# A decoder layer's two feed-forwards: gate and up as seven block products, tokens in two halves, rounds unrolled

## The chip, the cores and the metric

The kernel runs on one core of a Trainium2 chip. The metric is the device time of one execution in microseconds (us); lower is better. The work of a core is split over TensorE (PE: matrix products, with the weight loads as rows of their own, PEld), VectorE (DVE), ScalarE (ACT), GpSimd (POOL) and SyncE (SP: issues transfers). The engines run their own instruction lists in order and meet at semaphores (`wait_ge`, `then_inc`).

## The reference

One layer of a hybrid decoder for 1024 prompt tokens and 64 sample tokens (together NT = 1088), model width D = 1024. The change is about the two feed-forwards that open and close the layer, each with D_FF = 2816:

```
x += 0.5 * SwiGLU(rms(x))
gate, up = split(rmsnorm(x, g) @ w_in, 2)      # w_in: 1024 x 5632
SwiGLU   = (silu(gate) * up) @ w_out           # w_out: 2816 x 1024
```

Between them lie the projection of x into the inputs of three branches (sparse attention, a gated recurrence, attention to a memory), the branches, and their merge by `w_out`. These parts stay, but for the norm in front of the projection and the order of the merge's last products.

## The kernel before

All activations lie transposed in SBUF: `x[:, k, t]` holds feature 128k+partition of token t, k = 0 to 7 (KT = 8). The tokens stand in three chunks `CH` of 364, 362 and 362 columns. Products keep float32 accuracy by splitting each factor into a rounded high part and a remainder: `products` (L325) issues three matmuls for each 128x128 block of weights, `w_hi*a_hi`, `w_hi*a_lo`, `w_lo*a_hi`, and sums them in PSUM.

`Feed` (L336) is a feed-forward. A Fori loop has G = 11 rounds; a round makes 256 of the 2816 inner features as two tiles t = 0, 1 and then multiplies by the two matching blocks of `w_out`:

- Weights come in six units of 128x1024 (gate and up of tile 0, of tile 1, two blocks of `w_out`). SP loads unit u into `raw` slot u % 3, ACT rounds it into `w_hi` (`high_part`, L472), POOL subtracts, `w_lo = raw - w_hi` (`low_part`, L386).
- `unit` (L397) on PE: for each chunk, 8 values of k times three matmuls, into PSUM banks 0 to 2 (gate) or 3 to 5 (up). A tile has 2 x 3 x 24 = 144 matmuls.
- `dve_products` (L507) on DVE scales the two by the tokens' inverse root (`sg`, `up`, one PSUM operand each), multiplies after ACT's silu (`pr`, both operands in SBUF) and, after ACT's rounding into `a_hi`, subtracts for `a_lo` (both in SBUF).
- `down` (L431): 24 groups (3 chunks x 8 rows j) of 6 matmuls, 144 in a round, each added into x by `dve_add` (L547), one PSUM operand and one in SBUF.

The norm does not stand in front of the products: `h_hi` and `h_lo` are x times gain, split; the inverse root (`Rooted`, `RootedWhole`, `RootedTiles`, L194 to L323) is worked out meanwhile and multiplied in behind. The norm in front of the projection, `NormBehind`, squares and sums each chunk after the last `dve_add` of its rows. The order is written out by hand on each engine; there is no planner.

## Time and profile before

| | |
|---|---|
| median of 3 runs | 3192.61 us (3187.55 to 3192.62) |
| span of the profiled execution | 3181.2 us |
| what the median has around the span | 11.4 us |
| mean granted TensorE clock | 0.986 of full speed |
| HBM read, written | 226.20 MB, 37.05 MB (83 GB/s over the span) |

The span reaches from the first to the last instruction of one execution; the runs' times are of other executions and take in what lies around it. No time of its own is given for the profiled execution beside its span. A group's "mean" is that of one instruction; matmuls overlap, so that the distance between their starts, not their duration, is what one costs. "Idle before" is the time that the engine stood before these instructions, with what ended it.

### The profile page before, as it was taken

To read this page: it belongs to the slowest core of one execution; us is meant where nothing else is said; L and a number is where in the kernel's file an instruction comes from. 1 tells how busy PE (TensorE), PEld (TensorE's weight loads), DVE (VectorE), ACT (ScalarE), POOL (GpSimd) and SP (SyncE) were. 2 spreads that over 40 slices of the span, in tenths; PEclk is the share of its full clock that TensorE was granted. 3 is DMA by queue.
4 is the path that set the end of the run, shared out by engine and by line. 5 is a ranking of instruction groups with operands and counts; after the bars stand their busy time and mean duration, and the time that the engine had idled before them with its cause. 6 is when DMAs were issued, how large, how long until landed. Compare 5 with 4: busy or idle time off the path is not lost. (4 is left out here: it accounts for less than half of the span.)

```text
span 3181.2 us, 51686 instructions
## 1 busy us (share of the span) xinstructions
PE 3076.4 (97%) x19690; PEld 2901.0 (91%) x19690; DVE 1736.2 (55%) x3041; ACT 911.5 (29%) x1616; POOL 667.9 (21%) x415
## 2 busy tenths in 40 slices
PE   8999999999899999999899999999999999999999
PEld 8999999999899999999756666679999999999998
DVE  6333333333669999999635666655544333333333
ACT  5111111111433333333344545441232111111111
POOL 2112221221453421133250000012112122121120
PEclk9999999999999999999989999999999999999999
DMA  3111111111223222222346556444421111111111
GB/s 117 47 40 40 53 41 45 46 40 47 86 77 92 86 74 86 61 74 66 100 159 207 179 171 203 151 161 144 130 61 41 46 46 40 46 46 40 40 49 60
DMA packets 256495, 265.47 MB, mean 83 GB/s; under 512 B 14575, under 2 KB 197458, under 8 KB 256334
## 3 DMA queue, kind: packets, MB, share of 16 engines
q1 hardware_dynamic: 250858, 254.61, 25.6%
q0 software_dynamic: 4128, 4.20, 0.5%
q10 hardware_dynamic: 1348, 4.49, 0.4%
q8 instruction: 103, 1.69, 0.2%
q14 instruction: 58, 0.48, 0.0%
HBM read 226.20 MB, written 37.05 MB: 83 GB/s over the span
## 5 line engine op out<-in xcount | busy, mean ns | idle before, releaser
L331 PE MATMUL bank<-h_hi,w_hi 128*128 128x362 f32 (+1 forms) x3384 | 1118.6, 331 | 19.6 <-DVE h_lo L218 6.4
L331 PE MATMUL bank<-h_lo,w_hi 128*128 128x362 f32 (+1 forms) x3384 | 1112.9, 329 | 0.0
L331 PE MATMUL bank<-h_hi,w_lo 128*128 128x362 f32 (+1 forms) x3384 | 1111.7, 329 | 0.0
L331 PEld LDWEIGHTS bank<-h_hi,w_hi 128*128 128x128 f32 x3384 | 638.3, 189 | 26.8 <-issue 11.9
L331 PEld LDWEIGHTS bank<-h_lo,w_hi 128*128 128x128 f32 x3384 | 638.8, 189 | 2.7
L331 PEld LDWEIGHTS bank<-h_hi,w_lo 128*128 128x128 f32 x3384 | 638.6, 189 | 0.0
L388 POOL TENSOR_TENSOR w_lo<-raw,w_hi 128x1024 fp32r<-128x1024 f32 x132 | 316.1, 2403 | 1267.3 <-ACT w_hi L483 1267.3
L553 DVE SCALAR_TENSOR_TENSOR x<-bank,x 128x362 f32<-128x362 f32 (+1 forms) x528 | 279.8, 534 | 212.1 <-PE bank L331 211.9
L331 PE MATMUL bank<-a_hi_ffn,w_hi 128*128 128x362 f32 (+1 forms) x1056 | 347.7, 329 | 7.3 <-DVE x L553 5.6
L331 PE MATMUL bank<-a_lo_ffn,w_hi 128*128 128x362 f32 (+1 forms) x1056 | 346.4, 328 | 0.0
L331 PE MATMUL bank<-a_hi_ffn,w_lo 128*128 128x362 f32 (+1 forms) x1056 | 346.2, 328 | 0.0
L516 DVE TENSOR_TENSOR sg_ffn<-bank,drs_ffn 128x364 f32<-128x364 f32 x132 | 70.3, 535 | 388.0 <-PE bank L331 387.6
L521 DVE TENSOR_TENSOR up_ffn<-bank,drs_ffn 128x364 f32<-128x364 f32 x132 | 70.6, 535 | 370.0 <-PE bank L331 370.0
L483 ACT CAST w_hi<-raw 128x1024 fp32r<-128x1024 f32 x132 | 135.8, 1044 | 428.6 <-PE bank L331 428.6
L1313 POOL TENSOR_TENSOR w_lo<-raw,w_hi 128x1024 fp32r<-128x1024 f32 x53 | 129.6, 2444 | 392.5 <-ACT w_hi L1537 392.5
L331 PEld LDWEIGHTS bank<-a_hi_ffn,w_hi 128*128 128x128 f32 x1056 | 198.4, 188 | 10.0 <-DVE x L553 7.8
L331 PEld LDWEIGHTS bank<-a_lo_ffn,w_hi 128*128 128x128 f32 x1056 | 198.5, 188 | 0.1
L331 PEld LDWEIGHTS bank<-a_hi_ffn,w_lo 128*128 128x128 f32 x1056 | 198.5, 188 | 0.0
L499 ACT CAST a_hi_ffn<-pr_ffn 128x364 fp32r<-128x364 f32 x132 | 65.6, 497 | 432.5 <-DVE pr_ffn L528 432.5
L3066 POOL TENSOR_TENSOR w_lo<-raw,w_hi 128x1024 fp32r<-128x1024 f32 x20 | 50.0, 2503 | 606.0 <-ACT w_hi L3115 606.0
L493 ACT ACTIVATE sg_ffn<-sg_ffn 128x364 f32<-128x364 f32 x132 | 66.7, 508 | 384.0 <-DVE sg_ffn L516 383.9
L1902 DVE MAX8 top<-S 128x8 f32<-128x384 f32 (+5 forms) x192 | 171.1, 891 | 4.1
(371 smaller groups left out, 4105.2 us busy)
## 6 DMA issues: line engine op xcount, KB each, us to landing
raw<-in_w_ffn_in SPq DMA_DIRECT2D x88, 512.0 KB, 3.8
k_ring<-in_cache_k SPq DMA_DIRECT2D x128, 256.0 KB, 3.9
v_ring<-in_cache_v SPq DMA_DIRECT2D x128, 256.0 KB, 4.3
raw<-in_w_in SPq DMA_DIRECT2D x53, 512.0 KB, 4.8
raw<-in_w_ffn_out SPq DMA_DIRECT2D x44, 512.0 KB, 3.5
kept_g<-stage SPq DMA_DIRECT2D x24, 544.0 KB, 3.1
gate<-kept_g SPq DMA_DIRECT2D x24, 544.0 KB, 3.6
x<-x_kept SPq DMA_DIRECT2D x8, 544.0 KB, 4.5
```

Of the source, the lines that this page charges most:

```text
L331: mm = pe.matmul(out, left, right, start=(start and i == 0 and j == 0), stop=(stop and i == n - 1 and j == 2))
L388: pool.tensor_tensor(self.w_lo[:, u % 3, :], self.raw[:, u % 3, :], self.w_hi[:, u % 3, :].bitcast(F32), ALU.subtract).then_inc(self.low, 1)
L483: act.copy(self.w_hi[:, u % 3, :], self.raw[:, u % 3, :]).then_inc(self.high, 1)
L493: act.activation(self.sg[:, c, 0:w], self.sg[:, c, 0:w], ACT.Silu).then_inc(self.silu_done, 1)
L499: act.copy(self.a_hi[:, t, t0:t0 + w], self.pr[:, c, 0:w]).then_inc(self.prod_high, 1)
L516: dve.tensor_tensor(sg[:, c, 0:w], bank[c][:, 0:w], rs[:, t0:t0 + w], ALU.mult).then_inc(self.scaled, 1)
L521: dve.tensor_tensor(up[:, c % 2, 0:w], bank[3 + c][:, 0:w], rs[:, t0:t0 + w], ALU.mult).then_inc(self.up_scaled, 1)
L553: dve.scalar_tensor_tensor(self.x[:, j, t0:t0 + w], bank[:, 0:w], 0.5, self.x[:, j, t0:t0 + w], ALU.mult, ALU.add).then_inc(self.x_added, 1)
L1313: pool.tensor_tensor(w_lo[:, n % 3, :], raw[:, n % 3, :], w_hi[:, n % 3, :].bitcast(F32), ALU.subtract).then_inc(low, 1)
L1902: after(dve.max(top8[0:rows, :], scores))
L3066: pool.tensor_tensor(w_lo[:, n % 3, :], raw[:, n % 3, :], w_hi[:, n % 3, :].bitcast(F32), ALU.subtract).then_inc(low, 1)
```

## The change

The tokens are taken in two halves, `HV`: 512 tokens as two column blocks of 256, then 576 as two of 288. All 11 rounds are run for the first half, then for the second (ROUNDS = 22, written out, no loop), so every weight is loaded and split twice.

For a tile, gate and up are one 2x2 block product: rows gate and up, inner halves k = 0 to 3 and 4 to 7, columns the two token blocks. It is made with seven block products in place of eight (the form with 4 + 4 operand sums and 7 sums of results). The four sums of activation blocks (T1 to T4) are made once for each half, by DVE, with their high and low parts (`Operands`; three of the seven low parts by POOL). These operands are of the fully normed x, so the inverse root is needed before the first product. The four sums of weight blocks (S1 to S4, 128x512 each) are made for each tile by DVE (`combine`). The weights are split in 18 pieces of 512 columns for each round (7 + 7 + 4), through a ring of 10. The results are put together by an ACT copy (`first_copy`) and seven DVE additions (`post`), each with one PSUM operand. `down` has 8 rows j, each of two column blocks, 96 matmuls in a round.

The norm before the projection does its first chunk during the last rounds, the merge's last products are split 512, 288, 288 and reordered, four of the nine row tiles of the result are written during the second feed-forward's second half, and the start transposes and squares tile by tile.

```diff
+HV = [(0, 256), (512, 288)]
+OPS = 7
+B11, T2, B21, T3, T1, T4, B22 = range(OPS)
+PIECES = 18
+A11, S2, A12, S3, S1, A22, S4 = range(OPS)
+BANK_OF = (0, 1, 0, 1, 3, 2, 3)
+FIRST = (0, 4, 1, 2, 3, 5, 6)
+POSTS = 7
+POST_OF = (1, 2, 3, 4, 4, 5, 6)
...
+    def high_part(self, act, p):
...
+        if p >= self.RING:
+            i0, n0 = divmod(p - self.RING, PIECES)
+            if n0 < 14:
+                act.wait_ge(self.multiplied, self.after(2 * i0 + n0 // OPS, n0 % OPS))
+            else:
+                act.wait_ge(self.out_ready, KT * i0 + (4 if n0 < 16 else 8))
+        act.copy(self.ring_hi[p % self.RING], self.source(p)).then_inc(self.high, 1)
+    def low_part(self, pool, p):
+        pool.wait_ge(self.high, p + 1)
+        pool.tensor_tensor(self.ring_lo[p % self.RING], self.source(p), self.ring_hi[p % self.RING].bitcast(F32),
+                           ALU.subtract).then_inc(self.low, 1)
+    def combine(self, dve, g, m):
...
+        if g:
+            dve.wait_ge(self.low, self.piece(g - 1, m) + 1)
...
+        dve.tensor_tensor(s(m), left, right, op).then_inc(self.combined, 1)
+    def product(self, pe, g, n):
...
+        pe.wait_ge(self.low, p + 1)
...
+        if n == 2:
+            pe.wait_ge(self.first_copied, g + 1)
+        elif n == 3:
+            pe.wait_ge(self.posted, POSTS * g + 1)
+        elif n == 6:
+            pe.wait_ge(self.posted, POSTS * g + 5)
...
+    def on_act(self, act, hooks):
...
+                for n in range(OPS):
+                    if n == 0:
+                        self.first_copy(act, g)
+                    elif n == 2:
+                        self.silu(act, g, 0)
+                    elif n == 6:
+                        self.act_prod_high(act, g, 0)
+                        self.silu(act, g, 1)
+                        self.act_prod_high(act, g, 1)
+                    hooks(act, i, t, n)
+                    self.high_part(act, at + n)
...
+    def tile_on_dve(self, dve, g, ahead):
+        some = (lambda m: self.combine(dve, g + 2, m)) if ahead else (lambda m: None)
+        self.post(dve, g, 0)
+        some(S3)
+        self.post(dve, g, 1)
+        some(S1)
+        self.post(dve, g, 2)
+        some(S2)
+        self.post(dve, g, 3)
+        self.post(dve, g, 4)
+        some(S4)
+        self.post(dve, g, 5)
+        self.gate_up(dve, g, 0)
+        self.post(dve, g, 6)
+        self.prod_low_part(dve, g, 0)
+        self.gate_up(dve, g, 1)
+        self.prod_low_part(dve, g, 1)
...
+    def on_dve(self, dve, hooks, before_adds, after_add):
+        for i in range(self.ROUNDS):
+            self.tile_on_dve(dve, 2 * i, True)
+            self.tile_on_dve(dve, 2 * i + 1, False)
+            hooks(dve, i)
+            turn = i == self.G - 1
+            if turn:
+                self.next_half_early(dve)
+                self.next_half(dve)
+            for m in (S3, S1, S2):
+                self.combine(dve, 2 * i + 3, m)
...
+            for j in range(KT):
+                self.add(dve, i, j)
...
+                if j == 4 and not turn:
+                    self.combine(dve, 2 * i + 3, S4)
```

In `on_dve`, `next_half_early` and `next_half` make the second half's operands: eight scalings of 576 columns, and sums and low parts of 1152 columns, of which the later ones stand between and behind the eight additions of the round.

## Rows read from the trace of the kernel before

**Rows 1.** The page: busy time of each engine, share of the span, instructions

```profile
PE 3076.4 (97%) x19690; PEld 2901.0 (91%) x19690; DVE 1736.2 (55%) x3041; ACT 911.5 (29%) x1616; POOL 667.9 (21%) x415
```

**Rows 2.** Tile a_hi_ffn, two rounds: count, ns min/median/max, first and last start

```profile
L331 PE MATMUL bank<-a_hi_ffn,w_hi x48: 323/329/330, 291.1 to 314.6; 128*128 128x362 f32 x32, 128*128 128x364 f32 x16
...
L331 PE MATMUL bank<-a_hi_ffn,w_hi x48: 322/329/330, 721.7 to 745.1; 128*128 128x362 f32 x32, 128*128 128x364 f32 x16
```

**Rows 3.** Timeline of TensorE, 256 columns: start us, duration us

```profile
1671.82 0.28 PE L331 MATMUL bank<-w_hi,m_lo 128*128 128x256 f32 x1
...
1673.50 0.28 PE L331 MATMUL bank<-w_hi,m_hi 128*128 128x256 f32 x1
```

**Rows 4.** Busy time, clock and DMA in six stretches

```profile
core 0: us, PE busy (x) PEld busy (x) DVE busy (x) ACT busy (x) POOL busy (x), PEclk, DMA share, GB/s
315.00:386.70 71.70, 71.70 (x434) 71.70 (x433) 25.17 (x48) 11.81 (x18) 14.35 (x6) 1.00 0.15 44
47.50:50.00 2.50, 0.79 (x4) 0.29 (x3) 2.47 (x3) 1.89 (x3) 0.00 (x0) 1.00 0.00 0
824.50:842.00 17.50, 10.84 (x46) 9.45 (x45) 14.06 (x16) 7.43 (x14) 8.75 (x7) 0.71 0.50 144
2267.00:2270.00 3.00, 0.88 (x6) 0.58 (x4) 2.93 (x7) 0.99 (x2) 0.00 (x0) 1.00 1.10 342
2270.00:2275.00 5.00, 4.14 (x16) 4.14 (x17) 2.23 (x5) 1.44 (x2) 2.37 (x1) 0.66 0.29 73
2364.50:2378.00 13.50, 8.00 (x28) 6.79 (x27) 12.94 (x18) 4.16 (x5) 4.96 (x2) 0.62 0.27 78
```

**Rows 5.** Groups by form (mean ns last before the bar), one by line (min/median/max)

```profile
L388 POOL TENSOR_TENSOR w_lo<-raw,w_hi 128x1024 fp32r<-128x1024 f32 x132 | 316.1, 2403 | 1267.3 <-ACT w_hi L483 1267.3
...
L483 ACT CAST w_hi<-raw 128x1024 fp32r<-128x1024 f32 x132 | 135.8, 1044 | 428.6 <-PE bank L331 428.6
...
L553 DVE SCALAR_TENSOR_TENSOR x<-bank,x 128x362 f32<-128x362 f32 x352 | 188.0, 534 | 161.3 <-PE bank L331 161.2
...
L2540 DVE COPY kt<-bank 128x512 f32<-128x512 f32 x64 | 44.3, 691 | 66.3 <-PE bank L2732 66.3
...
L1554 ACT CAST qq<-qi 64x512 fp32r<-64x512 f32 x12 | 7.4, 614 | 0.2
...
L2306 DVE RECIPROCAL mk_rs<-mk_rs x1: 6552/6552/6552, 1653.4 to 1653.4; 128x1024 f32<-128x1024 f32 x1
```

**Rows 6.** Lines L3189, L528 and L553: ns min/median/max, who waited

```profile
L3189 DVE TENSOR_TENSOR m_lo<-m,m_hi x24: 527/531/2445, 2224.8 to 2271.2; 128x362 fp32r<-128x362 f32 x16, 128x364 fp32r<-128x364 f32 x8
...
  PE bank L331: 3.0, 1
...
L528 DVE TENSOR_TENSOR pr_ffn<-sg_ffn,up_ffn x132: 535/536/2717, 55.9 to 3141.9; 128x362 f32<-128x362 f32 x88, 128x364 f32<-128x364 f32 x44
...
L553 DVE SCALAR_TENSOR_TENSOR x<-bank,x x528: 520/535/538, 80.2 to 3170.6; 128x362 f32<-128x362 f32 x110, 128x364 f32<-128x364 f32 x66
```

**Rows 7.** Timelines of VectorE and GpSimd at 2224 us

```profile
2224.81 2.38 DVE L3189 TENSOR_TENSOR m_lo<-m,m_hi 128x364 fp32r<-128x364 f32 x1 [0.96 <-PE bank L331]
...
2224.39 2.40 POOL L3066 TENSOR_TENSOR w_lo<-raw,w_hi 128x1024 fp32r<-128x1024 f32 x1 [10.19 <-ACT w_hi L3115]
```

**Rows 8.** GpSimd line L985, and VectorE's timeline while it runs

```profile
L985 POOL TENSOR_TENSOR nss_mix<-nss_mix,nsq_mix x18: 827/973/1121, 799.9 to 842.8; 128x362 f32<-128x362 f32 x12, 128x364 f32<-128x364 f32 x6
...
842.96 1.16 DVE L1026 TENSOR_TENSOR h_lo<-nhn_mix,h_hi 128x362 fp32r<-128x362 f32 x1
```

**Rows 9.** Tiles h_hi and a_hi_ffn: both feed-forwards' first and last products

```profile
L331 PE MATMUL bank<-h_hi,w_hi x96: 322/329/609, 18.2 to 73.2; 128*128 128x362 f32 x64, 128*128 128x364 f32 x32
...
L331 PE MATMUL bank<-a_hi_ffn,w_hi x48: 322/329/605, 794.4 to 824.2; 128*128 128x362 f32 x32, 128*128 128x364 f32 x16
...
L331 PE MATMUL bank<-h_hi,w_hi x96: 321/329/674, 2367.7 to 2423.0; 128*128 128x362 f32 x64, 128*128 128x364 f32 x32
...
L331 PE MATMUL bank<-a_hi_ffn,w_hi x48: 322/329/412, 3142.1 to 3169.9; 128*128 128x362 f32 x32, 128*128 128x364 f32 x16
```

More of the change, by code:

```diff
@@ new lines, in on_pe, with first_copy @@
+    def on_pe(self, pe, hooks, after_down):
+        for i in range(self.ROUNDS):
+            for t in range(2):
+                for place, n in enumerate(self.order(2 * i + t)):
+                    hooks(pe, i, t, place)
+                    self.product(pe, 2 * i + t, n)
+            self.down(pe, i, after_down if i == self.ROUNDS - 1 else None)
+    def first_copy(self, act, g):
+        i, t = divmod(g, 2)
+        w = HV[self.half(i)][1]
+        act.wait_ge(self.multiplied, self.after(g, 0))
+        if g:
+            act.wait_ge(self.posted, POSTS * (g - 1) + 2)
+        act.copy(self.s1[:, 0:w], self.bank[4 * t][:, 0:w]).then_inc(self.first_copied, 1)
```

1306 lines of the change are left out of this document (757 added, 549 removed).

## The prediction

> **What bounds the kernel now.** I read the page's busy times first: TensorE is busy 97% of the span, VectorE 55%, ScalarE 29%, GpSimd 21% [rows 1]. Then the windows by stage: in a steady round of the feed-forward PE has no gap at all (71.70 of 71.70 us, clock 1.00, which is 2.4 GHz), with DVE at 25.2 us, ACT at 11.8 and POOL at 14.4 [rows 4]. So there the time is that of the matmuls' issue, and nothing else. Six rounds take 721.7 - 291.1 = 430.6 us, 71.77 us each; with 432 matmuls in a round that is 0.1661 us for one of 362.67 columns [rows 2]. The two feed-forwards run from 18.2 to 824.2 us and from 2367.7 to 3169.9 [rows 9], 806 and 802 us; 11 rounds are 789.5, so 16.5 and 12.7 are their own starts and ends.
>
> **The matmuls.** What does a narrower one cost? The trace has the same triple of products with 256 columns: 14 steps in 1.68 us, 0.120 us each [rows 3]. It doesn't stop falling at 256, and the line through both points (0.43 ns a column, 9 ns fixed) gives 0.1338 us for 288. Gate and up: before 2 x 11 x 2 x 144 = 6336 matmuls, 1052.4 us; after 2 x 44 tiles x 84 = 7392, half at 0.120 and half at 0.1338, 938.0 us: **-114.4 us**, 10.9% and not 12.5%, since the fixed part is paid on more instructions. Down: before 3168, 526.2 us; after 2 x 22 x 96 = 4224, 536.0 us: **+9.8**. If nothing waits, the change is worth -104.6 us. A round is then 31.7 us (256) or 35.3 (288).
>
> **What the other engines get.** In these 31.7 us POOL has 18 subtractions of 512 columns. The trace has 362 columns at 0.827 us undisturbed and 1024 at 2.40 [rows 5, 8]; between them lies 1.18 us, so 21 us, 67% where it had 20%. DVE has 14 posts (0.42 us, from 0.534 for 362 and 0.691 for 512 [rows 5]), 8 combines of 512 (0.69), 8 products and low parts (0.42) and 8 additions of 512 (0.69): 20.3 us. ACT has 18 copies of 512 (0.61) and 10 of about 0.4 (from 0.614 and 1.044): 15 us [rows 5]. No engine is full. But the sums must not be read alone, for one thing that before hid by its timing.
>
> **DVE behind POOL.** The line m_lo L3189 takes 0.53 us in the median and 2.445 at most, L528 0.535 and 2.717 [rows 6]. Beside POOL's timeline: POOL starts at 2224.39 for 2.40 us, DVE's m_lo starts at 2224.81 and ends at 2227.19, 0.40 us after POOL's end [rows 7]. The same with short POOL instructions: 1.16 for 0.53 [rows 8]. The additions L553, whose one operand is PSUM, never exceed 0.538 in 528 [rows 6]. So a DVE instruction with both operands in SBUF that starts while POOL runs waits until POOL's instruction is done, then needs about its columns' time; and PE did wait for it (3.0 us [rows 6]). That this is so in general the Trainium skill says in "SBUF — State Buffer", Who interferes with whom: a DVE instruction with two SBUF inputs and a GpSimd instruction that reads SBUF share a port, and the second blocks fully; the trace agrees. Before, a round has 12 such DVE instructions and POOL runs 20% of the time. After, it has 16 in half the time, POOL runs 67%, and two of the combines wait for POOL's semaphore just when POOL goes on with its next piece.
>
> **A round by hand (256 columns, 0 = first product).** The end of down frees pieces 8 and 9; POOL does 8 to 11 back to back until 2.1, 3.3, 4.5 and 5.65. DVE's combine S3 overwrites the sum that piece 10 reads, is released at 4.5, meets piece 11 in POOL and ends at 5.65 + 0.55 = 6.2. Behind it: post 1 (6.6), silu (7.0), ACT's high part of 12 (7.5), POOL's 12 and 13 (9.1, 10.3). S4 is released by 13, meets 14 (until 11.45), ends 12.0; post 5 12.4; gate_up meets 15 and ends 13.2; post 6 13.6, silu 14.0, gate_up 14.5, ACT's rounding 14.95, high part of 16 15.5, and only then, in ACT's order, first_copy of tile 1: 15.8. PE started product 6 at 8.95 in place of 8.64 (post 4 late: 0.3), has done tile 1's products 0 and 1 at 13.3, and waits for the copy: **2.6 us**. In down the additions come behind three combines and cost another 0.5. Together 3.4 us in a round of the first half. With 288 columns PE is slower and the chain hardly: 0, 1.7 and 0.3, together 2.0. For 2 x 11 pairs of rounds: 22 x 5.4 = **+119 us**. PE has more work than this chain everywhere else; second tiles have no combines inside.
> Bounds: without DVE's waits behind POOL the same chain ends at 13.6 and costs 0.75 a round of 256 and 0.1 of 288, +19 us; with every hop 0.1 us longer and the waits a whole POOL instruction each, 4.8 and 3.2, +176 us.
>
> **The turn between the halves (twice).** Behind the last tile of half 1, DVE does 8 scalings of 576 columns (0.72 each, by the row of 512), a sum and a low part of 1152 (1.3 each), the three combines, 13.5 us in all since PE's last gate product, and only then the first addition that down's fifth group (due at 5.8) waits for: 8.5 us. The new half's first tile needs each 1152-column sum, high and low part in turn, some with POOL (2.7 each): 5 us more than a usual one. And a gap of 3 us on PE is followed by half clock: 0.66 over the 5 us from 2270, 0.62 over the 13.5 us from 2364.5 that begin with such a gap (the lower level is 1.2 GHz), while a gap of 2.2 us at 47.5 leaves it at 1.00 [rows 4]; here that is worth some 3.5 us. Together 17, **+34 us** (20 to 50).
>
> **Starts, seams, the rest.** First feed-forward: the first product now needs root, reciprocal (6.55 us for 1024 columns [rows 5], so 3.3 for 512), scaling, sum, high and low: at about 26 us, not 18.2 [rows 9], and the tile is some 7 us longer; together 15, and 4 for the projection's norm inside the last additions, against 16.5: **+2**. Second: first product some 4 us after the merge, a tile 8 us longer and 5 of slow clock, against 12.7 and the 3 us in front of it: **+1**. At the projection's start PE stands 6.7 of 17.5 us at clock 0.71 [rows 4], some 12 us lost; its first chunk's norm is now ready: **-8**. These are worth -20 to +20 together. The transfers double for the feed-forwards, to some 100 GB/s; windows with 342 exist [rows 4], each unit is asked for 15 us ahead: nothing. No loop: the instruction fetch lies under PE's work as it does in the projection, which is straight code: nothing.
>
> **Sum:** -104.6 + 119 + 34 - 5 = +43 us. Against the profiled execution's span of 3181.2 that is 3224; the median of the runs stands 11.4 above that span, so **3236 us**.
>
> **Rivals.**
> *A, the forecast:* PE waits for first_copied some 2 to 3 us in each round. Likeliest's own range 3205 to 3270. For it speak rows 6 to 8. Chance 0.45.
> *B, faster:* the waits of DVE behind POOL seldom fall on the chain to first_copy. Then 22 x 0.85 = 19 us of stalls, a turn of 12 each: 3192.6 - 104.6 + 19 + 24 - 5 = 3126. It decides from 3.4 us per pair of rounds: below it the kernel is faster. For it: in the whole trace of before few of such instructions are hit (medians 0.53 [rows 6]); against: POOL's share then and now. Chance 0.25.
> *C, the clock falls too:* the 2.6 us gap lies between 2.2 (kept) and 3 (lost). If each 256 round loses about 3.4 us at half clock, 1.7 us: 22 x 1.7 = +37, 3273. Chance 0.15. The Trainium skill ("TensorE: Matmul & The Clock Gate", HAM oscillation) tells of kernels in which each such wait is followed by half clock; no row of before shows a repeated one.
> *D, a longer chain:* the upper bound above, 8.0 us per pair: +176 in place of 119, 3293. Chance 0.15.
> That narrow matmuls aren't cheaper is excluded by rows 3.
>
> So slower by over 0.2% (which is about what a measurement of this kernel tells from no change) in A, C and D but for a little: 0.70; within 0.2% 0.05; faster 0.25. The range takes in B's centre and D with a margin: 3120 to 3320; about 0.1 is left below, 0.05 above.
>
> **What would show it.** Matmul starts 0.120 and 0.134 us apart; 7392 + 4224 in the feed-forwards. A PE wait of 1.5 to 3 us once in each round, released by ACT's first_copy; combines with a median near 1.2 us and posts at 0.42 to 0.46; rounds of 35 and 37 us; one hole of 8 us in each feed-forward's middle. The prediction is wrong if rounds are under 33 and 36 us, if the combines take 0.7 in the median, or if PE's clock falls in each round.

## The result, and the profile after

| | before | after |
|---|---|---|
| median of the runs | 3190.08 us (3186.04 to 3192.62, 4 runs) | 3425.39 us (3420.92 to 3428.33, 4 runs) |
| span of the profiled execution | 3181.2 us | 3422.8 us |
| mean granted TensorE clock | 0.986 | 0.951 |

The ratio is 1.0738 (95% interval 1.0723 to 1.0754). The forecast was slower, 3236 us, with a range up to 3320: the direction is right, the size is not. It said +43 us and the change costs 235 (242 between the two spans). The forecast also took 11.4 us as what stands around the span. The profiled execution of the changed kernel took 3424.36 us, only 1.6 above its span, so most of the 11.4 was the difference between two executions of the kernel before.

The page of the changed kernel, busy times; beside [rows 1] POOL's time has more than doubled and PE's share has fallen:

```profile
PE 3075.7 (90%) x21770; PEld 2870.5 (84%) x21802; DVE 2286.8 (67%) x3670; ACT 1281.6 (37%) x2445; POOL 1456.3 (43%) x1087
```

Windows of the changed kernel (rounds are counted from 0). They answer to [rows 4]: a steady round of 256 columns, one of 288, the second feed-forward's first round from its first product, the two rounds of its turn, and round 15 of the first feed-forward:

```profile
core 0: us, PE busy (x) PEld busy (x) DVE busy (x) ACT busy (x) POOL busy (x), PEclk, DMA share, GB/s
2743.10:2780.60 37.50, 33.82 (x267) 33.30 (x266) 23.10 (x38) 13.91 (x28) 24.07 (x18) 0.95 0.28 85
3069.20:3107.30 38.10, 36.02 (x270) 35.66 (x269) 24.50 (x38) 14.68 (x29) 23.73 (x18) 1.00 0.33 98
2529.70:2593.00 63.30, 42.70 (x269) 40.40 (x270) 48.05 (x54) 25.28 (x44) 45.21 (x28) 0.76 0.22 67
2930.80:2978.40 47.60, 36.47 (x267) 35.94 (x266) 33.13 (x50) 19.30 (x33) 20.76 (x16) 0.86 0.18 56
2978.40:3031.20 52.80, 41.35 (x267) 40.26 (x266) 33.17 (x42) 16.17 (x31) 36.34 (x24) 0.84 0.24 70
678.60:726.30 47.70, 40.10 (x266) 39.47 (x266) 28.13 (x38) 15.00 (x30) 27.46 (x20) 0.89 0.22 67
```

A round with nothing in its way takes 31.7 or 35.3 us. None does. The account of the 242 us, from the starts of each round's first product and of the stages' last products, beside the terms of the forecast:

| us | forecast | measured |
|---|---|---|
| products and `down` alone (taken over; run 1 bears it out) | -104.6 | -104.6 |
| steady rounds, over 31.7 and 35.3 | +101 | +211 |
| the turns' four rounds, over the same | +45 | +67 |
| starts, less before's own (30 in 806 and 802 us) | +10 | +66 |
| projection to merge | -8 | +5 |
| end | 0 | -2 |
| sum | +43 | +242 |

(The forecast's 5.4 us per pair of rounds are counted here in the row to which the round belongs. Steady rounds are the 38 that are neither first nor at a turn. Starts: the first feed-forward's first product stands at 40.4 in place of 18.2 us, the second's 12.0 behind the merge's last in place of 3.0, and the first rounds last 65.2 and 63.3 us from there.)

The forecast's chain is there. VectorE, GpSimd, ScalarE and TensorE at the end of the first tile of a round that begins at 2743.1 (columns: start us, duration us, in brackets the idle time ahead and what ended it):

```profile
2753.91 1.77 DVE L399 TENSOR_TENSOR sums_ffn<-raw,sums_ffn 128x512 f32<-128x512 f32 x1 [1.76 <-POOL w_lo L369]
2755.60 0.41 DVE L543 TENSOR_TENSOR up_ffn<-bank,u_ffn 128x256 f32<-128x256 f32 x1
2756.12 1.00 DVE L550 TENSOR_TENSOR sg_ffn<-sg_ffn,up_ffn 128x256 f32<-128x256 f32 x1
```

```profile
2753.85 2.99 POOL L369 TENSOR_TENSOR w_lo<-raw_ffn,w_hi 128x512 fp32r<-128x512 f32 x2
```

```profile
2758.39 0.40 ACT L498 CAST a_hi_ffn<-sg_ffn 128x256 fp32r<-128x256 f32 x1 [0.49 <-DVE sg_ffn L550]
2758.70 0.61 ACT L365 CAST more_hi_ffn<-raw_ffn 128x512 fp32r<-128x512 f32 x1
2759.22 0.36 ACT L483 COPY s_ffn<-bank 128x256 f32<-128x256 f32 x1
```

```profile
2759.73 0.36 PE L231 MATMUL bank<-op_hi_ffn,more_hi_ffn 128*128 128x256 f32 x1 [2.89 <-ACT s_ffn L483]
```

S4's combine starts 0.06 us behind GpSimd's piece and takes 1.77 us; `gate_up` takes 1.00; `first_copy` comes at 2759.22, 16.1 us into the round (forecast 15.8), and PE stands 2.89 us for it, 3.17 from start to start of its matmuls (forecast 2.6). With two more waits (product 6 and down's fifth group, 0.6 and 0.5 us longer than a matmul's step) and the clock at 0.95 the round lasts 37.5 us where 35.1 was forecast.

The combines of the changed kernel, ns min/median/max, to be set beside [rows 6]:

```profile
L399 DVE TENSOR_TENSOR sums_ffn<-raw x88: 674/688/1703, 25.1 to 3345.5; 128x512 f32<-128x512 f32 x88
...
L399 DVE TENSOR_TENSOR sums_ffn<-raw,sums_ffn x88: 681/1738/1771, 27.1 to 3372.7; 128x512 f32<-128x512 f32 x88
...
L399 DVE TENSOR_TENSOR sums_ffn<-raw_ffn x44: 671/1777/1786, 60.2 to 3366.8; 128x512 f32<-128x512 f32 x44
```

S4 (second line) is stretched in most places and tile 1's S1 (third line) in 36 of 44; of the first group one half is (S3 of tile 0, as forecast). What the forecast had not is how the wait is shared out: whichever instruction comes first keeps its time and the other engine's waits. In the rows above GpSimd's piece of 2753.85 keeps its 1.28 us, S4 behind it takes 1.77, and GpSimd's next piece, which meets S4, takes the rest of the 2.99. So GpSimd's 1.28 us become 1.5 to 1.75 as well wherever the two meet.

### The profile page after: what moved, and what is told of

The parts are those of the page before. It is cut to its first block and busy times, and to the rows that moved or that the text cites. A ratio compares the mean times of both kernels' runs of the same rounds, so it can differ in the third digit from the quotient of the medians.

```text
span 3422.8 us, 58318 instructions
## 1 busy us (share of the span) xinstructions
PE 3075.7 (90%) x21770; PEld 2870.5 (84%) x21802; DVE 2286.8 (67%) x3670; ACT 1281.6 (37%) x2445; POOL 1456.3 (43%) x1087
## 5 line engine op out<-in xcount | busy, mean ns | idle before, releaser
L231 PE MATMUL bank<-op_hi_ffn,w_hi 128*128 128x256 f32 (+1 forms) x1488 | 456.7, 307 | 137.1 <-ACT s_ffn L483 72.4
L231 PE MATMUL bank<-op_lo_ffn,w_hi 128*128 128x256 f32 (+1 forms) x1488 | 450.1, 302 | 0.0
L231 PE MATMUL bank<-op_hi_ffn,w_lo 128*128 128x256 f32 (+1 forms) x1488 | 448.8, 302 | 0.0
L231 PE MATMUL bank<-h_hi,w_hi 128*128 128x362 f32 (+1 forms) x1272 | 421.6, 331 | 8.9 <-ACT xp L1834 5.0
L231 PE MATMUL bank<-h_lo,w_hi 128*128 128x362 f32 (+1 forms) x1272 | 418.4, 329 | 0.0
L231 PE MATMUL bank<-h_hi,w_lo 128*128 128x362 f32 (+1 forms) x1272 | 418.0, 329 | 0.0
L3338 POOL TENSOR_TENSOR w_lo<-raw,w_hi 128x1024 fp32r<-128x1024 f32 x20 | 50.8, 2546 | 606.4 <-ACT w_hi L3391 606.4
L231 PEld LDWEIGHTS bank<-op_lo_ffn,w_hi 128*128 128x128 f32 x1488 | 303.8, 204 | 0.1
L231 PEld LDWEIGHTS bank<-op_hi_ffn,w_lo 128*128 128x128 f32 x1488 | 303.3, 204 | 0.0
L1575 POOL TENSOR_TENSOR w_lo<-raw,w_hi 128x1024 fp32r<-128x1024 f32 x53 | 129.3, 2441 | 383.9 <-ACT w_hi L1801 383.8
L231 PEld LDWEIGHTS bank<-h_hi,w_hi 128*128 128x128 f32 x1272 | 240.5, 189 | 13.1 <-issue 5.8
```

The costliest lines, as they stand in the source:

```text
L231: mm = pe.matmul(out, left, right, start=(start and i == 0 and j == 0), stop=(stop and i == n - 1 and j == 2))
L1575: pool.tensor_tensor(w_lo[:, n % 3, :], raw[:, n % 3, :], w_hi[:, n % 3, :].bitcast(F32), ALU.subtract).then_inc(low, 1)
L3338: pool.tensor_tensor(w_lo[:, n % 3, :], raw[:, n % 3, :], w_hi[:, n % 3, :].bitcast(F32), ALU.subtract).then_inc(low, 1)
```

## The experiments

Runs are numbered as they stand here. Each stands beside runs of the kernel before on the same chip; its ratio is to those. Differences between versions are differences of ratios times 3187; where two intervals overlap, the difference is not shown by the times and rests on the gaps in the traces alone.

### What a steady round waits for

**1. The lock itself**, that is DVE's waiting for GpSimd's reads. GpSimd writes what it otherwise computes.

```diff
-        pool.tensor_tensor(self.ring_lo[p % self.RING], self.source(p), self.ring_hi[p % self.RING].bitcast(F32),
-                           ALU.subtract).then_inc(self.low, 1)
+        pool.memset(self.ring_lo[p % self.RING].bitcast(F32), 0.0).then_inc(self.cleared, 1)
+        pool.wait_ge(self.cleared, p + 1)
+        pool.memset(self.ring_lo[p % self.RING].bitcast(F32), 0.0).then_inc(self.low, 1)
```

> Edit: POOL's low parts of the weights are left out; in their place POOL clears the 512 columns twice (two memsets, together about as long, 1.1 us for 1.3, but reading nothing from SBUF). Theory 1 (DVE instructions with two SBUF operands wait for POOL instructions that read SBUF): combine's median falls from about 1.7 to 0.69 us, S4 ends 2.5 us earlier, rounds 34 us (256, clock kept) and 36.5 (288): about -100 us, near 3325. Theory 2 (DVE is slow or late for another reason, POOL only in its own queue): combine keeps its duration, and less than 20 us is gained.

3204.01 us, ratio 1.0054 (1.0033 to 1.0075): 218 us less than the changed kernel, twice what theory 1 had. A steady round of each kind, and the combines:

```profile
core 0: us, PE busy (x) PEld busy (x) DVE busy (x) ACT busy (x) POOL busy (x), PEclk, DMA share, GB/s
2588.60:2620.40 31.80, 31.80 (x267) 31.76 (x265) 19.15 (x38) 14.09 (x28) 18.40 (x36) 1.00 0.33 100
2875.30:2910.90 35.60, 35.60 (x271) 35.60 (x270) 20.48 (x38) 14.96 (x29) 18.47 (x36) 1.00 0.35 105
```

```profile
L401 DVE TENSOR_TENSOR sums_ffn<-raw,sums_ffn x88: 681/683/694, 27.0 to 3155.6; 128x512 f32<-128x512 f32 x88
```

PE is busy without a gap, so 264 matmuls cost what the forecast gave them (0.120 and 0.134 us each), at twice the transfers' rate of before. POOL is still busy 58% of the round, now with writes of 0.53 us, and no combine is stretched: GpSimd's reading is what DVE waits for. This is what the Trainium skill says ("SBUF — State Buffer", Who interferes with whom): a DVE instruction with two SBUF inputs contends with one of GpSimd that reads, not with one that only writes. But POOL's chain is also shorter here (1.05 us a piece for 1.28 or more), so this run takes away the lock between the engines and the length together; run 4, with GpSimd's work unchanged, parts them.

**2. ScalarE's order.** Tile 1's `first_copy` is issued ahead of silu 1 of tile 0.

```diff
                         self.act_prod_high(act, g, 0)
+                        if t == 0:
+                            self.first_copy(act, g + 1)
                         self.silu(act, g, 1)
```

> Edit: in tile 0 of each round ACT issues tile 1's first_copy ahead of silu 1 and of the last rounding, not behind them and piece 16's high part. Theory 1 (PE's wait of 3.17 us at tile 1's third product is ACT's order, fed by the DVE chain): the wait falls under 1 us, PE's clock no longer falls in the 256 rounds, rounds go from 37.5 to about 33.5 us (256) and from 38.1 to 36 (288): about -120 us, near 3305. Theory 2 (the chain is long whatever ACT does): the wait moves to tile 1's fourth product, which needs post 0 behind the last low part, or into down; then 35.5 and 37.5, about -50 us.

3409.33 us, 1.0701 (1.0680 to 1.0722): -12. The wait for the copy falls from 3.17 to 1.4 us, and waits of 0.6 us at the next product and 2.4 us (from 0.64) at down's fifth group take its place. That is less than either theory had: the 256 rounds of the second feed-forward take 36.6 us, or 38.1 where half clock follows the new wait (five of nine). The queue ahead of the copy is not the cause; DVE is late with everything behind it.

**3. DVE's order.** Each combine one or more posts later, S4 at the tile's end.

```diff
         self.post(dve, g, 0)
-        some(S3)
         self.post(dve, g, 1)
-        some(S1)
+        some(S3)
         self.post(dve, g, 2)
-        some(S2)
+        some(S1)
...
-        some(S4)
+        some(S2)
...
         self.prod_low_part(dve, g, 1)
+        some(S4)
```

> Edit: on DVE, combine S3 stands behind post 1, S1 behind post 2, S2 behind post 4, S4 behind the tile's last low part; nothing else is changed. Theory 1 (S3 and S4, which wait for POOL's semaphore and then for its next piece, hold up the posts): post 5 starts when its product is done, the wait at tile 1's third product falls from 3.17 to about 1 us, rounds 34 (256) and 36 us (288): -110 us. Theory 2 (the time is DVE's total): S4 now delays tile 1's post 0, and the wait appears at tile 1's fourth product: about -30 us.

3331.18 us, 1.0455 (1.0433 to 1.0477): -90 by four moved lines, near theory 1's 110. Rounds of 34.7 and 36.8 us; the wait for the copy is 1.2 us and the clock stays at 1.00 in all steady rounds of the second feed-forward. The combines still meet GpSimd; they only no longer stand in front of a post or a product that PE waits for.

**4. Operands in PSUM.** The same arithmetic, but tile 0's `up` and gated product stay in banks that are free by then (post 4 into the bank of products 1 and 3, post 5 and `gate_up` in place; `gated` gives bank 2 or 1 for tile 0, `sg` for tile 1), so that four DVE instructions have one PSUM operand in place of two in SBUF.

```diff
+        if t == 0 and n in (4, 5):
+            to = self.bank[1 if n == 4 else 2][:, 0:w]
...
+        at = self.gated(g, c)
+        up = self.up[:, c * w:(c + 1) * w] if g % 2 else at
+        dve.tensor_tensor(at, sg, up, ALU.mult).then_inc(self.prod_done, 1)
```

> On the changed kernel, same arithmetic. Tile 0's up values and gated products are left in PSUM (post 4 into the bank of the third product, post 5 in place, gate times up in place), so that the four DVE instructions of tile 0 behind silu (two gate_up, two low parts) have one PSUM operand and should not wait for GpSimd. Theory 1, DVE behind GpSimd on the chain to tile 1's first_copy: gate_up 1.0 and 1.0 become 0.42, the PE wait in front of tile 1's third product falls from 3.17 us to under 2.0 in the rounds of 256 columns and the clock no longer falls there; round 37.5 to 35 us, 288 columns 38.07 to 37.3: -50 to -70 us, 3365. Theory 2, the combines alone set the chain: gate_up is not what is late, the gap stays over 2.8 us and the time falls by less than 15 us.

3385.18 us, 1.0625 (1.0607 to 1.0643): -36, between the two theories. `gate_up` of both tiles, ns mean before the last bar:

```profile
L554 DVE TENSOR_TENSOR sg_ffn<-sg_ffn,up_ffn 128x256 f32<-128x256 f32 x44 | 22.9, 520 | 2.3
...
L554 DVE TENSOR_TENSOR bank<-sg_ffn,bank 128x256 f32<-128x256 f32 x44 | 18.9, 429 | 2.3
```

Tile 0's is 429 ns (0.60 us over both tiles before), under GpSimd's reads and at unchanged POOL work, so it is the operands' place that decides. The wait for the copy goes from 3.17 to 2.57 us, by the 0.57 that the one `gate_up` on its chain had lost (1.00 to 0.43). Two neighbouring rounds with this wait, one at full clock and one not:

```profile
core 0: us, PE busy (x) PEld busy (x) DVE busy (x) ACT busy (x) POOL busy (x), PEclk, DMA share, GB/s
2613.80:2649.70 35.90, 32.34 (x267) 31.82 (x266) 23.04 (x39) 13.85 (x28) 24.04 (x19) 1.00 0.30 90
2649.70:2686.60 36.90, 33.83 (x267) 33.31 (x266) 22.53 (x39) 13.87 (x28) 23.91 (x19) 0.95 0.29 87
```

In this run the wait of 2.55 to 2.57 us is followed by 3.4 us at half clock in 13 of the 16 rounds that have it, and such a round is 1.0 us longer.

**5. Both, 3 and 4.** No other edit.

> The kernel of the run with the combines moved later (3331 us) with tile 0's up values and gated products in PSUM as well, same arithmetic. Theory 1: both remove different waits behind GpSimd on the same chain; the 1.20 us gap in front of tile 1's third product falls to about 0.3 and the round of 256 columns from 34.7 to about 33.7, that of 288 from 36.8 to 36.0: -32 us, 3299. Theory 2: with the combines late, the chain is no longer bound there but by the additions at down's fifth group (1.45 us), which then grow: -10 us or less, 3321 or more.

3288.48 us, 1.0328 (1.0311 to 1.0345): -40 against run 3, a little more than theory 1 had. The steady rounds:

```profile
core 0: us, PE busy (x) PEld busy (x) DVE busy (x) ACT busy (x) POOL busy (x), PEclk, DMA share, GB/s
2552.50:2586.10 33.60, 32.17 (x266) 31.80 (x265) 23.43 (x38) 14.06 (x28) 24.88 (x18) 1.00 0.32 95
2952.10:2987.90 35.80, 35.80 (x271) 35.64 (x270) 23.20 (x38) 14.84 (x29) 24.58 (x18) 1.00 0.35 104
```

With all of POOL's reading left in, rounds of 288 columns have no wait over 0.3 us, and those of 256 have 1.44 us in front of down's fifth group and 0.55 at product 6.

### The first feed-forward's norm

**6 and 7.** GpSimd's sums left out but for one column (run 6), and the whole sums at another place (run 7):

```diff
+        m = 1 if c == 0 else w
-        pool.tensor_tensor(self.ss[:, t0:t0 + w], self.ss[:, t0:t0 + w], self.sq[:, n % 3, 0:w], ALU.add
+        pool.tensor_tensor(self.ss[:, t0:t0 + m], self.ss[:, t0:t0 + m], self.sq[:, n % 3, 0:m], ALU.add
```

> On the changed kernel. GpSimd's seven sums of squares for the projection norm's first chunk, made during rounds 12 to 16 of the first feed-forward, add one column in place of 364; the rest of each sum is left out. Theory 1, GpSimd's time: the 5.1 to 5.5 us that PE stands in front of down's fifth group in rounds 13 to 16 come from GpSimd being about 1 us a sum late with the weights of the next pieces and from DVE's instructions behind these sums; without them the four gaps fall to 1 us or less and half of their half-clock time goes: 4 x (4.5 + 2.5) = 28 us, 3397. Theory 2, ScalarE: the squares on ScalarE (0.5 us each, two a round) and the wait for the additions keep the roundings back; the gaps stay over 4 us and the time is 3420 or more.

3413.01 us, 1.0711 (1.0693 to 1.0729): -9, not told apart from the changed kernel by the times. The four gaps fall from 5.1 to 5.5 us to 4.2 and no further, so the sums' own time is the small part. Run 7 has what keeps them.

```diff
-        if n == 0 and 0 <= k < 4:
+        if n == 4 and 0 <= k < 4:
```

> On the changed kernel, same arithmetic. In rounds 13 to 16 of the first feed-forward GpSimd makes the norm's two sums ahead of the next round's piece 4 in place of piece 0. Theory 1, the order: in the trace of the changed kernel GpSimd stands idle from about 701 to 703.2 us with pieces 0 to 3 ready, since its next instruction is a sum that waits for ScalarE's squares, which stand in ScalarE's order behind the fifth product of tile 1; the four pieces come some 4 us late and every DVE instruction of tile 1 then meets GpSimd. With the sums at piece 4 the gap in front of down's fifth group falls from 5.5 to 1 to 2 us and most of the half clock goes: 4 x 6.5 = -26 us, 3399. Theory 2, the added work (two sums, two squares) is what costs: the gaps stay over 4 us and the time within 8 us of 3425.

3402.87 us, 1.0667 (1.0645 to 1.0690): -23. The gaps are 0.8 to 1.5 us, the rounds 38.5 to 40.8 in place of 44.0 to 47.7. GpSimd in the changed kernel had stood 5.6 us for ScalarE's squares:

```profile
703.22 2.29 POOL L1212 TENSOR_TENSOR nss_mix<-nss_mix,nsq_mix 128x364 f32<-128x364 f32 x2 [5.59 <-ACT nsq_mix L1204]
```

Pieces that ScalarE had rounded by then stood behind that wait, as theory 1 had it. Two sums of 1 us cost 8.5 us a round, 6.2 of it by where they stood.

### The turn and the starts

**8. GpSimd's share of the operands** left out, without a read:

```diff
+        if o in (B21, T4, B22):
+            eng.memset(self.lo[s][:, o, :, :].bitcast(F32), 0.0).then_inc(self.low[1], 1)
+            return
```

> On the changed kernel. GpSimd's three low parts of the activation operands (three for each half of each feed-forward, 12 in all) are left out: GpSimd clears the places by one memset each, without reading SBUF; the low parts of the weights stay. Theory 1, the lock in the starts and turns: GpSimd's 2.5 to 3.4 us instructions stretch DVE's sums and low parts of 1024 columns from 1.2 to 2.2 to 3.4 us, some five of them in a start and two or three in a turn. Then each start gets 6 to 8 us shorter with the clock and each turn 3: about -20 us, 3405. Theory 2: the starts are the chain of the operands itself on DVE (8 scalings, 4 sums, 4 low parts, 16 us alone) and GpSimd's weight pieces stretch it as much: the time falls by under 8 us.

3409.30 us, 1.0695 (1.0677 to 1.0713): -14. First rounds are 3.2 us shorter, the second round of each turn 5.1. Nearer theory 1, but a tenth of what starts and turns cost.

**9. Four additions ahead of the operands' second half** in the turn:

```diff
             for j in range(KT):
                 self.add(dve, i, j)
+                if turn and j == 3:
+                    self.next_half(dve)
+                    for m in (S3, S1, S2):
+                        self.combine(dve, 2 * i + 3, m)
```

> Edit: at the turn between the halves the first four additions of down stand ahead of the second four scalings and the three combines, and the sum T2 and low part T1 behind the fifth. Theory 1 (PE's 8.1 us gap in down at the turn is the additions behind the operand making): the gap falls to about 2.5 us, and 5 us are gained at each turn, -10 us. Theory 2 (DVE is the bound of the turn as a whole): the gap moves to the first products of the second half, less than 3 us gained.

3422.74 us, 1.0744 (1.0723 to 1.0764): nothing. The wait in `down` falls from 8.1 to 3.2 us and the round from 47.6 to 41.6; the next goes from 53 to 58.0 and 59.5. Theory 2: what one round wins the next one pays.

**10. Repairs together**: run 5, the sums at piece 4, and the 3.7 us reciprocal cut in two behind the additions of rounds 7 and 8.

```diff
-        if i == 8:
-            ops.dve_invert(dve, 1)
...
+            if i in (7, 8) and self.late_invert:
+                self.ops.dve_invert_part(dve, i - 7)
```

> Same arithmetic. The run with tile 0's products in PSUM and the combines late (3288 us), with the norm's sums at piece 4, and with the reciprocal for the second half (3.7 us on DVE ahead of round 8's additions) cut into two of 288 columns behind the additions of rounds 7 and 8, where DVE waits for the next tile. Theory 1: rounds 13 to 16 fall from 42.5 to 36 us and round 8 from 39.6 to 34: -30 us, 3258. Theory 2: the reciprocals now meet the next round's first posts and combines and the norm's sums the pieces behind them: -12 us or less, 3276 or more.

3261.13 us, 1.0231 (1.0207 to 1.0255): -31 against run 5. Rounds 13 to 16 take 36.4 us, round 8 33.6. What is left stands in starts and turns. The second feed-forward's start in this kernel, VectorE and then TensorE:

```profile
2450.15 3.74 DVE L180 RECIPROCAL op_rs_ffn<-op_rs_ffn 128x576 f32<-128x576 f32 x1
2453.81 0.62 DVE L410 TENSOR_TENSOR sums_ffn<-raw,raw_ffn 128x512 f32<-128x512 f32 x1
...
2456.54 0.42 DVE L556 TENSOR_TENSOR u_ffn<-bank,s_ffn 128x256 f32<-128x256 f32 x1
```

```profile
2457.10 0.55 PE L241 MATMUL bank<-op_hi_ffn,w_hi 128*128 128x256 f32 x1 [8.66 <-DVE u_ffn L556]
```

Post 0, which PE waits for, stands behind a reciprocal that is needed some 360 us later and behind four combines. In the turn ScalarE's `first_copy` stands behind the rounding of a late sum:

```profile
2843.48 2.21 ACT L215 CAST op_hi_ffn<-op_f_ffn 128x1152 fp32r<-128x1152 f32 x2 [6.61 <-DVE op_f_ffn L208]
...
2846.63 0.39 ACT L494 COPY s_ffn<-bank 128x288 f32<-128x288 f32 x1
```

**11. The order at these places** (reciprocal into rounds 7 and 8 in both feed-forwards; tile 1's combines behind posts 1 and 4; in the turn `first_copy` ahead of two roundings and S4 behind post 1):

```diff
-        ops.dve_invert(dve, 1)
-        for s in (S3, S1, S2, S4):
-            feed.combine(dve, 1, s)
...
+            if i == self.G - 1:
+                self.first_copy(act, 2 * self.G)
+                for o in (T3, B22):
+                    self.ops.act_high(act, 1, o)
```

> The repaired kernel (3261 us), same arithmetic, with only the order changed in each feed-forward's first tile and in the turn: the reciprocal of the second half stands behind the additions of rounds 7 and 8 in the second feed-forward too, tile 1's combines stand behind post 1 and post 4 in place of ahead of post 0, and in the turn ScalarE's first_copy stands ahead of two of the operands' roundings and S4's combine behind post 1. Theory 1, order: in the trace before it PE stands 8.9 us in front of the fourth-placed product of the second feed-forward, until post 0 at 2456.5, which stands behind a reciprocal of 3.7 us and four combines of 0.7; in the turn 5.8 us for first_copy at 2846.6, which stands behind the rounding of a sum that DVE makes late, and 3.3 us for post 0 behind S4's combine. Then the second start gets 6 us shorter, the first 3, each turn 6: -21 us, 3240. Theory 2, sheer DVE work: the combines and posts only change places, PE waits later in the same tile: -6 us or less.

3253.07 us, 1.0209 (1.0191 to 1.0227): -7, theory 2's number, with intervals that overlap. The 8.9 us at the fourth-placed product are 2.6 and the turn's 5.8 are gone, but 4.2 to 4.9 us stand in front of tile 1's fourth product, which waits for post 0 behind the combines that now stand at tile 0's end. The old order had been the cause of the wait; the new one made another.

**12. The additions ahead of three combines.**

```diff
-            for m in (S3, S1, S2):
+            for m in (S3, S1, S2) if turn else ():
...
                 self.add(dve, i, j)
+                if j in (1, 2, 3) and not turn:
+                    self.combine(dve, 2 * i + 3, (S3, S1, S2)[j - 1])
```

> The order-fixed kernel with the three combines S3, S1, S2 of the next round's second tile moved from ahead of down's additions to behind the second, third and fourth of them (not in the turn). Theory 1: the gap of 1.45 us in front of down's fifth group in the rounds of 256 columns is the time by which these combines, 1.7 us each behind GpSimd, make the first addition late; it goes: 17 x 1.3 and a few us from rounds 1 to 3, 13 to 16 and 20, -25 us against the order-fixed kernel. Theory 2: the combines now meet the next tile's first posts and products 6 and 9 wait for them: -8 us or less.

3214.40 us, 1.0095 (1.0076 to 1.0114): -36 against run 11, more than theory 1's 25. Steady rounds are 32.3 and 35.6 us:

```profile
core 0: us, PE busy (x) PEld busy (x) DVE busy (x) ACT busy (x) POOL busy (x), PEclk, DMA share, GB/s
2585.70:2618.00 32.30, 32.02 (x267) 31.82 (x266) 23.06 (x39) 14.06 (x28) 25.02 (x18) 1.00 0.33 99
2911.50:2947.10 35.60, 35.60 (x270) 35.60 (x269) 22.08 (x40) 14.84 (x29) 24.73 (x18) 1.00 0.30 90
```

POOL reads as much as ever and DVE is as busy as in the changed kernel (23.1 us). So 5.2 us of the changed kernel's 37.5 were order and the place of two operands, with the clock that followed.

**13. The combines that run 11 had put at the first tile's end**, spread over the second tile (the third place in which they stand):

```diff
+        elif g % (2 * self.G) == 1:
+            for m in (S3, S1, S2):
+                self.combine(dve, g + 1, m)
...
+        if g % (2 * self.G) == 1:
+            self.combine(dve, g + 1, S4)
```

> The run with the additions first (3214 us), same arithmetic, with the four combines for the third tile of each half moved from the end of the first tile to behind post 1 (three) and the last low part (one) of the second tile. Theory 1, order: the gap of 4.6 to 4.9 us in front of the fourth product of the second tile, which waits for post 0 behind these four combines (6.4 us behind GpSimd), goes in all four places: -4 x 4.5 = -18 us, 3196. Theory 2: DVE has no slack there and the wait moves on to the seventh product or to down: -6 us or less.

3200.98 us, 1.0058 (1.0041 to 1.0074): -12, between the theories. The gaps of 4.6 to 4.9 are gone; in their place come 0.6 to 2.4 us later on. The turn's second rounds fall from 50.1 and 50.3 us to 45.1 and 47.1.

**14. The turn's three combines behind its fifth addition.**

```diff
-            for m in (S3, S1, S2) if turn else ():
-                self.combine(dve, 2 * i + 3, m)
...
+                if turn and j == 4:
+                    for m in (S3, S1, S2):
+                        self.combine(dve, 2 * i + 3, m)
```

> The kernel with the combines spread, and in the turn the three combines that stand ahead of down's additions placed behind the fifth of them. Theory 1: the gap of 8.9 us in front of down's fifth group in the turn falls by their 2.1 us, and with the first_copy ahead it doesn't come back: -2 x 2 = -4 us. Theory 2, DVE is full in the turn (2817 to 2846 us in the trace of the repaired kernel without a pause): the next tile loses what down wins, within 2 us.

3200.12 us, 1.0048 (1.0034 to 1.0062): no change. The turn's first round is 2.6 to 2.9 us shorter and the second 2.1 to 4.1 longer. This order buys nothing in the turn; that of run 13 did.

### The clock by itself

**15.** Idle matmuls inside PE's waits, into the bank that the next product overwrites:

```diff
+            count = (30 if self.spare else 20, 8, 0, 25, 18, 0, 8) if g == 0 else (0, 0, 20, 10, 0, 0, 8)
+            for _ in range(count[n]):
+                pe.matmul(self.bank[BANK_OF[n]][:, 0:P], self.ops.ones[:, :], self.ops.ones[:, :], start=True, stop=True)
```

> The kernel of the run before in this list with idle matmuls (128x128 of ones, written to the bank that the next product then overwrites) issued on PE inside its waits: 20 and 30 ahead of the feed-forwards' first products, 18, 8, 25 and 8 ahead of four products of the first tile, and 20, 10 and 8 in the second half's first tile. Nothing else changes. Theory 1, the clock is a cost of its own: 37 to 43 us at half clock in each feed-forward's first round and 10 to 14 us in each of the two rounds of a turn give half of themselves back where PE, not the operands, is last; starts -8 each, turns -5 each: -26 us, 3232. Theory 2: in starts and turns DVE's operands are last until the first tile's end, so that a faster PE only waits longer: within 8 us of the kernel without the filler.

3265.10 us, 1.0240 (1.0213 to 1.0268), run 10 having 1.0231: no gain. The start and the turn's second round:

```profile
core 0: us, PE busy (x) PEld busy (x) DVE busy (x) ACT busy (x) POOL busy (x), PEclk, DMA share, GB/s
2414.30:2496.50 82.20, 63.33 (x474) 61.18 (x473) 59.53 (x69) 27.96 (x48) 45.81 (x28) 0.88 0.20 59
...
2842.20:2894.20 52.00, 46.21 (x343) 45.38 (x342) 32.62 (x42) 16.80 (x31) 37.37 (x24) 0.93 0.24 72
```

In run 10 the same two had clocks of 0.76 and 0.90 and lasted 77.6 and 51.5 us. In the turn the clock is up a little (3.4 us less at half clock) and the time is not shorter. The start shows nothing, by a fault of mine: the idle matmuls in front of the fourth-placed product stood behind its wait for post 0 and took 8.1 us there. Run 16 leaves them out.

**16.** On run 13's kernel, with idle matmuls only ahead of a feed-forward's first three products:

```diff
+            count = (30 if self.spare else 20, 8, 0, 0, 18, 0, 0) if g == 0 else (0,) * OPS
```

> The kernel of the run above with idle matmuls on PE only where an operand's low part is awaited: 20 or 30 ahead of a feed-forward's first product, 18 and 8 ahead of the next two. Theory 1, the clock: PE reaches the first tile's later products at full clock, 35 to 40 us of half clock a start become under 15, and since the later waits are shorter than before half of that is given back: -8 us a start, -16 us against the run above. Theory 2: operands are still last until the first tile's end; what is gained is the second tile and down at full clock only: -4 us or less.

3196.60 us, 1.0040 (1.0026 to 1.0054) beside 1.0058 (1.0041 to 1.0074) for run 13: not to be told apart, where theory 1 had -16. First rounds 74.5 and 74.2 us beside 75.1 and 73.1, though the half clock in them fell from 37 and 31 us to 19 and 17. Theory 2: DVE's operands are last until the first tile's end; a faster PE waits longer.

**17. The bound without the lock**: run 15 with the weights' low parts left out:

> The filler kernel with the weights' low parts left out (GpSimd clears each place twice by memset in their place, without reading SBUF). It bounds what is left of the lock between DVE and GpSimd in the repaired kernel. Theory 1: rounds of 256 columns fall from 33.6 to 31.8 us (18 of them), those of 288 from 35.8 to 35.2 (20), starts by 5 us each: -55 us against the filler kernel, about 3180, so that starts and turns alone then eat the 105 us that the products save. Theory 2: the repairs have already removed nearly all of the lock's cost: less than 25 us below the filler kernel.

3201.36 us, 1.0043 (1.0030 to 1.0056): -63 against its filler kernel, theory 1's number and more. Rounds are of 31.7 and 35.1 to 35.6 us. Even so it is not faster than before, and run 13, with all of the work in it, has since come as far.

**18. The last version**: run 16 with DVE's side work behind the additions and silu's table loaded in a pause.

```diff
-            hooks(dve, i)
             turn = i == self.G - 1
...
+            hooks(dve, i)
...
+            act.activation(ops.eps[:, :], ops.eps[:, :], ACT.Silu)
```

> The last filler kernel (3197 us), same arithmetic. DVE's side work of a round (one sum of squares, in round 0 the constants as well) stands behind the round's additions in place of ahead of them, and in the second feed-forward a silu of one column on ScalarE, in a pause ahead of the first tile's last two operand roundings, takes the 1.28 us of loading silu's table off the chain to the second tile. Theory 1: the gap of 5.4 us in round 0 of the first feed-forward goes to under 1 (-6 us with its half clock), the gap of 3.0 us in front of the second feed-forward's tenth product to 1.7 (-2 us): 3189, within 0.2% of the kernel before. Theory 2: the sum and the constants then stand ahead of the next tile's posts, and the second tile waits for its products' posts, not for the table: -3 us or less.

3192.60 us, 1.0018 (1.0010 to 1.0027; 12 runs beside 17). Both gaps went as expected (5.5 to 1.0, 3.0 to 1.6), but the first came back as 3.2 us in the next round's first tile, by theory 2, and the second in part at the tile's end. The best version stands within 0.2% of the kernel before, and by its interval above it.

## Why the forecast was right, and where it failed

Of the 199 us between +43 and +242, the steady rounds hold 110, the starts 56, projection to merge 13, the turns 22 and the end -2. The path that the forecast rests on was there (rival A, with C and D beside it). But C and D added to it give 3330; the rest stood in no rival.

**The matmuls: right.** 31.8 us for a round without waits (run 1) where 31.7 was forecast, 35.6 where 35.3 was.

**DVE behind POOL: right in mechanism and place.** Run 1 takes the reads away, run 4 the second SBUF operand, and runs 3, 5 and 12 move the instructions that pay. The reading of [rows 6] to [rows 8] holds, with one correction: DVE isn't alone in paying. Where the two meet, GpSimd's own piece goes from 1.28 us to 1.5 to 1.75, and I had costed 1.18 for it from [rows 5, 8], where it takes 1.28 undisturbed. By my reading that made every hop longer; no run shows it by itself. The chain gave 4.2 us of waits in a 256 round where 3.4 was forecast, 2.8 with 288 where 2.0 was. With single rounds' oddities that is some 33 of the 110 us missed in the steady rounds, what the next two items leave.

**The clock: rival C was true and I gave it 0.15.** In the changed kernel the wait of 3.17 us is followed by 3.4 us at half clock in all 16 rounds that have it (0.95 in the window above), the 2.4 us of the second feed-forward's 288 rounds in 2 of 8. That is 16 rounds by 1.7 us and two by 1.5, some 30 us. The 2.6 us that I had forecast would mostly not have kept the clock either: run 4 has such waits, and 13 of its 16 are followed by half clock. What the trace before shows of single gaps, 2.2 us kept and 3 us lost [rows 4], did not tell what repeated ones do. Counted net it is 1.0 us a round (run 4: 36.9 beside 35.9), since at full clock the wait at down's fifth group is 1.1 us in place of 0.6. The Trainium skill ("TensorE: Matmul & The Clock Gate", HAM oscillation) tells of a kernel in which the waits for transfers, mostly longer than these, are each followed by half clock; the 3.17 us waits here agree. In starts and turns more of the clock bought nothing that could be told (runs 15 and 16), where the forecast had 3.5 us a turn for it.

**The side work inside the rounds: not in the forecast**, but for 4 us. Three pieces of it in the steady rounds were passed over: the early sums of rounds 13 to 16 (34 us, of which run 7 got 23 back by moving them), the reciprocal in round 8 (6), and root and table load in round 18 (6). Each stands in front of an instruction with no slack now that the rounds have none. That makes 46 us.

**"Starts, seams, the rest: -5" is the step that failed worst.** In the table's terms +66 and +5 stand where +10 and -8 were forecast. The chain was priced with undisturbed durations (0.72, 1.3, 3.3) and to its first product: 26 us, where it came at 40.4. TensorE's and VectorE's rows on this chain in the changed kernel:

```profile
24.59 2.07 PE L166 MATMUL bank<-op_ss_ffn,ones 128*128 128x512 f32 x2 [9.67 <-DVE op_ss_ffn L879]
...
31.17 5.76 DVE L188 SCALAR_TENSOR_TENSOR op_f_ffn<-x,par,op_rs_ffn 128x512 f32<-128x512 f32 x4
36.96 2.18 DVE L198 TENSOR_TENSOR op_f_ffn<-op_f_ffn 128x1024 f32<-128x1024 f32 x1
...
40.42 0.55 PE L231 MATMUL bank<-op_hi_ffn,w_hi 128*128 128x256 f32 x1 [10.34 <-DVE op_lo_ffn L213]
```

Beside GpSimd three of the four scalings take 1.75 us for 0.75, and the sum 2.18 for 1.22: 4 us, and run 1's first product comes 4.1 us earlier. The larger part is that the matmuls that sum the squares stand only at 24.6; my own durations for what follows add up to some 9 us, so 26 had them at 17, and no term of mine says why. Then the first tile goes on through more waits (5.3, 5.8, 3.2 and 1.8 us between starts of matmuls in the first feed-forward, and 6.1 in `down`, behind the constants), since DVE makes the operands one behind the other, at up to 3.4 us each beside GpSimd, with the posts behind them. The projection's start gained nothing to be seen.

**The turn: 17 forecast, 25 measured over two usual rounds.** Its first part (8.5 us late additions) was exact: 8.1 us. The second round was costed at 5 us over a usual one, with 3.5 of clock for both; it takes 14.7 more, 3 to 5 of them by the order that run 13 changed.

**The sign hung on order.** Run 13 computes the same and is 217 us faster, by order, the reciprocal's place and four operands in PSUM. What then remains outweighs what the products save by little: its feed-forwards take 796 and 795 us (806 and 802 before), 18 us won, and the later first products (21 and 9 us) with 4 us elsewhere take 35. How much of this is sheer operand work on DVE is open. For the turn, runs 9 and 14 show two orders that win nothing, and run 13 one that does. For the starts the clock is bounded (run 16), and a part is the lock: with GpSimd not reading the weights (run 1) they are 13 and 10 us shorter than in the changed kernel, from the matmuls that sum the squares to the second round.

## What to carry to other kernels

Before a change that adds DVE instructions with two SBUF operands and GpSimd reads, write the order of both engines out and ask which of the contended instructions stands in front of one that TensorE waits for: moving lines was worth some 170 of 242 us here (runs 3, 7, 11 to 13), a free PSUM bank for an operand 36 to 40. Cost a fill or a turn (a norm, operands, first products) to the end of its first round and not to its first product, and once for each time the change repeats it; here the starts and turns together (133 us) ate more than the 105 us saved. Side work that was free in a round with slack has to be priced again when the slack is gone.

## What the hardware showed that I had not expected

- DVE with two SBUF operands and GpSimd reading SBUF wait for each other by turns: a DVE instruction of 0.69 us takes 1.74 to 1.78, and GpSimd's of 1.28 takes up to 1.75. I had read a one-sided wait from the trace of before.
- A wait of 2.55 us, once a round of 36.9, is followed by half clock in most rounds (13 of 16, run 4), where a single gap of 2.2 us in the trace of before was not.
- A GpSimd memset of 512 columns takes 0.53 us and doesn't stretch DVE's combines (0.681 to 0.694 us for S4, run 1).
- The reciprocal takes 3.35 us for 512 columns and 3.74 for 576, as long as five combines; known from [rows 5], but not that it would stand in front of a product three times.
- Twice the half-clock time in a first round (37 us beside 19, runs 13 and 16) made no difference to its length that could be told.
